# Queries of the expert retrieval in three passes over split operands, in a two-layer encoder kernel on one core

## What is computed

```python
def block(xb):                                   # per block of tokens, 8 heads
    q = (xb @ w_query).reshape(t, PEER_HEADS, 2, PEER_HALF).astype(jnp.float32)
    scores = jnp.einsum('thpd,hpnd->thpn', q, sk)        # 2 x 128 keys per head
    s_val, s_idx = lax.top_k(scores, PEER_TOPK)
    cand = s_val[:, :, 0, :, None] + s_val[:, :, 1, None, :]
    c_val, c_idx = lax.top_k(cand.reshape(t, PEER_HEADS, PEER_TOPK * PEER_TOPK), PEER_TOPK)
    ...                                          # expert = i1 * 128 + i2
    gate = jax.nn.softmax(c_val, axis=-1)
    act = jax.nn.gelu(jnp.einsum('thkd,td->thk', expert_u[expert], xb).astype(jnp.float32))
    coef = (gate * act).astype(xb.dtype)
    return jnp.einsum('thk,thkd->td', coef, expert_v[expert])
```

## Time and profile before

| | us |
|---|---|
| median of 3 runs | 2816.58 (2815.05 to 2818.69) |
| the profiled execution, its own time | 2819.95 |
| span in its profile | 2818.1 |
| TensorE busy | 2798.6 (99%) |
| VectorE busy | 2334.7 (83%) |
| ScalarE busy | 1050.3 (37%) |
| granted TensorE clock, mean | 0.997 |

### The profile page before, as it was taken

One profiled execution on the slowest core, in us unless ns is written; L12 is line 12 of the kernel. 1 busy time (PEld: TensorE's weight loads), 2 busy tenths in 40 slices (PEclk: granted clock), 3 DMA queues, 4 the chain that ended last, 5 costly groups with the idle time before them and its releaser, 6 DMA issues.

```text
span 2818.1 us, 40542 instructions
## 1 busy us (share of the span) xinstructions
PE 2798.6 (99%) x15010; PEld 1575.0 (56%) x15010; DVE 2334.7 (83%) x4382; ACT 1050.3 (37%) x1394; POOL 747.8 (27%) x519
## 2 busy tenths in 40 slices
PE   9999999999999999999999999999999999999999
PEld 5455555556666444444467775555566664444444
DVE  5954899997888899999843568999978889999996
ACT  2163323234555333333442442323345553333332
POOL 0000233421111445445200002333301114545450
PEclk9999999999999999999999999999999999999999
DMA  4213578776997999999702246878679979999993
GB/s 160 90 47 128 216 268 300 269 280 248 316 313 269 395 393 400 400 390 397 288 34 90 77 155 248 311 260 308 248 267 315 313 294 400 399 395 394 400 396 145
DMA packets 213943, 776.06 MB, mean 275 GB/s; under 512 B 14484, under 2 KB 101016, under 8 KB 193848
## 3 DMA queue, kind: packets, MB, share of 16 engines
q1 hardware_dynamic: 49200, 416.89, 38.6%
q0 software_dynamic: 73728, 268.47, 25.5%
q10 hardware_dynamic: 90888, 89.14, 9.4%
HBM read 681.90 MB, written 92.54 MB: 275 GB/s over the span
## 4 chain that ended last, share of the span: by engine, by line
PE 74%; issue 10%; PEld 8%; DVE 4%; DVEq 2%; ACT 1%; DMA 1%; PEldq 1%; POOL 0%; ACTq 0%; SPq 0%
PE ps L1983 15%; PE ps L1914 12%; PE ps L1913 12%; PE ps L1912 12%; PE ps L1886 8%; PEld ps L1983 8%; DVE arena L988 2%; PE ps L1588 2%; PE ps L1965 2%; PE ps L1964 2%; PE ps L1537 1%; PE ps L1538 1%; PE ps L1541 1%; DVEq L996 1%; PE ps L1922 1%
## 5 line engine op out<-in xcount | busy, mean ns | idle before, releaser
L1983 PE MATMUL ps<-arena 128*128 128x512 bf16 x4584 | 990.5, 379 | 1.7 <-DVE arena L1365 1.3
L521 POOL DMA_INDIRECT arena<-in_ur,arena x256 | 349.5, 1365 | 1548.7 <-DVE arena L1203 929.4
L1983 PEld LDWEIGHTS ps<-arena 128*128 128x128 bf16 x4584 | 448.2, 98 | 542.8 <-issue 1.7
L1176 DVE TENSOR_TENSOR arena<-arena 128x1024 bf16<-128x1024 f32 x512 | 611.7, 1220 | 117.0 <-ACT arena L767 95.3
L1914 PE MATMUL ps<-xnh,arena 128*128 128x384 bf16 x2048 | 667.6, 326 | 0.0
L1913 PE MATMUL ps<-xnl,arena 128*128 128x384 bf16 x2048 | 667.5, 326 | 0.0
L1912 PE MATMUL ps<-xnh,arena 128*128 128x384 bf16 x2048 | 667.4, 326 | 0.0
L767 ACT ACTIVATE arena<-arena 128x1024 bf16<-128x1024 f32 x512 | 524.7, 1048 | 122.8 <-PE ps L1983 99.6
L521 POOL DMA_INDIRECT arena<-in_v,arena x256 | 396.2, 1548 | 404.9 <-DVE x_res L1212 344.0
L1212 DVE SCALAR_TENSOR_TENSOR x_res<-arena,x_res 128x1024 f32<-128x1024 f32 x256 | 328.6, 1283 | 21.1 <-issue 0.9
L793 ACT ACTIVATE arena<-ps 128x384 f32<-128x384 f32 x256 | 125.6, 491 | 563.6 <-PE ps L1914 560.8
(11 more groups left out here) (250 smaller groups left out, 2544.8 us busy)
## 6 DMA issues: line engine op xcount, KB each, us to landing
arena<-in_v SPq DMA_DIRECT2D x64, 2048.0 KB
arena<-in_u SPq DMA_DIRECT2D x62, 2048.0 KB
h_scratch<-arena ACTq DMA_DIRECT2D x60, 768.0 KB
arena<-h_scratch SPq DMA_DIRECT2D x60, 768.0 KB
arena<-gate_scratch SPq DMA_DIRECT2D x64, 640.0 KB
arena<-in_wmix SPq DMA_DIRECT2D x14, 2048.0 KB, 7.9
gate_scratch<-xnT ACTq DMA_DIRECT2D x10, 2048.0 KB
gate_scratch<-arena ACTq DMA_DIRECT2D x10, 2048.0 KB
```

The lines of the kernel that those rows point to most:

```text
L521: pool.indirect_dma_start(ring[n % NBUF], None, ur_d[L] if g < P else vr_d[L], at).then_inc(gat_in[n % NBUF], 16)
L1176: dve.tensor_tensor(lo[:, s], raw[s // TPG][:, s % TPG], hi[:, s], ALU.subtract).then_inc(lo_ready, 1)
L1983: last = pe.matmul(ps[:, 2 + 2 * tt + dh], c, v[:, TPG * s + q, dh * 512:(dh + 1) * 512], start=start and c is ch and v is hi, stop=stop a ...
```

## The change

- The queries are made of rounded operands in three passes. x_hi (the rounded tokens) takes the place of xnT, x_rest (what is left) lies where x_res was. Before that, x goes to DRAM (x_keep, stored by ScalarE behind the norm's root, x_kept), and it is loaded again by SP after the last u group was asked for (x_back, waited for by VectorE at value group 4).
- The weights of a head are rounded by ScalarE into wq_hi (query_high: two activations of 128x1024, at the entry for head 0, then after the tile 8h + 4), and VectorE leaves the rest in the place of wq (query_low: two subtractions, in head h at a fixed place for head h + 1).
- TensorE makes per head 8 x 2 matmuls high x high and as many high x rest, in turn, and then 8 x 2 of low x high (high_tokens, low_weights). In head 0 the rests of tiles 2 and 3 are used only behind the first dense tile (rest_tokens), and the scores of head 0 come behind the second.
- norm_low and norm_high of tiles 1 to 3 write into xs; query_rest copies from there into x_hi and subtracts; the bf16 split reads xs too. For tile 0 the rests are eight operations out of PSUM.
- VectorE splits two tiles of u at once (split_two), except the first six of a layer.
- The one-hot rows are written two instructions in place of four, each twice as wide. Their order in the tile changes.

```diff
@@ -210,6 +212,10 @@
+        x_rest = rounded("x_rest", ARENA + KD * T + KD * TD, TT, KD, P)
+        wq_lo = rounded("wq_lo", A_X, KD, 2 * P)
+        wq_hi = [rounded("wq_hi0", A_X + 2304, KD, 2 * P)] + [rounded("wq_hi1", A_GR, KD, 2 * P)] * (PH - 1)
...
@@ -452,6 +463,10 @@
+                sp.wait_ge(q_done, PH * (L + 1))
+                for tt in range(TT):
+                    sp.dma_start(x[:, tt], x_keep[tt]).then_inc(x_back, 16)
...
@@ -548,6 +563,8 @@
+                if k % 2:
+                    act.dma_start(x_keep[tt], x[:, tt]).then_inc(x_kept[tt], 16)
...
@@ -766,8 +785,16 @@
+            def query_high(L, h):
+                act.wait_ge(wq_in, 16 * (PH * L + h + 1))
+                for p in range(2):
+                    at = slice(4 * p, 4 * p + 4)
+                    act.activation(wq_hi[h][:, at], wq[:, at], ACT.Copy).then_inc(q_high, 1)
+                query_high(L, 0)
...
@@ -834,6 +861,8 @@
+                    if n % RING == 4 and n < NK // 2 - RING:
+                        query_high(L, n // RING + 1)
...
@@ -925,15 +956,45 @@
+            def query_rest(k, tt):
+                at = slice(tt * P, (tt + 1) * P)
+                dve.wait_ge(xt_low, TT * k + tt + 1)
+                dve.drain()
+                if tt:
+                    src = xs[:, tt].rearrange("p (k t) -> p k t", t=P)
+                    dve.tensor_copy(x_hi[:, :, at], src).then_inc(x_top, 1)
+                    if tt == TT - 1:
+                        split_tile(tt)
+                    dve.wait_ge(x_kept[tt], 16 * (k // 2 + 1))
+                    dve.drain()
+                    dve.tensor_tensor(x_rest[:, tt], src, x_hi[:, :, at].bitcast(F32), ALU.subtract).then_inc(xt_rest, 1)
+                    return
+                dve.wait_ge(x_kept[tt], 16 * (k // 2 + 1))
+                for kd in range(KD):
+                    first = kd % (KD // 2) * P
+                    last = dve.scalar_tensor_tensor(x_rest[:, tt, kd], ps[:, turn_bank(k, tt) + kd // (KD // 2), first:first + P],
+                                                    cols[:, C_GAIN + KD * k + kd:C_GAIN + KD * k + kd + 1],
+                                                    x_hi[:, kd, at].bitcast(F32), ALU.mult, ALU.subtract)
+                last.then_inc(xt_rest, 1)
+            def query_low(L, h):
+                for p in range(2):
+                    at = slice(4 * p, 4 * p + 4)
+                    dve.wait_ge(q_high, 2 * (PH * L + h) + p + 1)
+                    dve.tensor_tensor(wq_lo[:, at], wq[:, at], wq_hi[h][:, at].bitcast(F32), ALU.subtract).then_inc(q_low, 1)
+            def split_tile(tt):
+                src, at = xs[:, tt].rearrange("p (k t) -> p k t", t=P), slice((tt - GT) * P, (tt - GT + 1) * P)
+                dve.tensor_copy(xnh[:, :, at], src)
+                dve.drain()
+                dve.tensor_tensor(xnl[:, :, at], src, xnh[:, :, at], ALU.subtract).then_inc(xn_split, 1)
-                if tt >= GT:
-                    dve.wait_ge(xt_low, TT * k + tt + 1)
-                    src, at = xnT[:, :, tt * P:(tt + 1) * P], slice((tt - GT) * P, (tt - GT + 1) * P)
-                    dve.drain()
-                    dve.tensor_copy(xnh[:, :, at], src)
-                    dve.drain()
-                    dve.tensor_tensor(xnl[:, :, at], src, xnh[:, :, at], ALU.subtract).then_inc(xn_split, 1)
+                query_rest(k, tt)
+                if GT <= tt < TT - 1:
+                    split_tile(tt)
...
@@ -947,6 +1008,8 @@
+                    if step == 2:
+                        query_low(m, 0)
...
@@ -1175,12 +1238,24 @@
+            def split_two(n, s, first):
+                if first is not None:
+                    dve.wait_ge(raw_in[s // TPG], first)
+                dve.wait_ge(hi_ready, n + 2)
+                at = slice(s % TPG, s % TPG + 2)
+                dve.tensor_tensor(lo[:, s:s + 2], raw[s // TPG][:, at], hi[:, s:s + 2], ALU.subtract).then_inc(lo_ready, 2)
-                    if n < TPG:
-                        dve.wait_ge(first_in[n], 16 * (L + 1))
-                    split_lo(T0 + n, n % RING, arrival(L, n) if n >= TPG and n % TPG == 0 else None)
+                    if n < AHEAD:
+                        if n < TPG:
+                            dve.wait_ge(first_in[n], 16 * (L + 1))
+                        split_lo(T0 + n, n % RING, arrival(L, n) if n == TPG else None)
+                    elif n % 2:
+                        n -= 1
+                        split_two(T0 + n, n % RING, arrival(L, n) if n % TPG == 0 else None)
...
@@ -1259,6 +1334,8 @@
+                    if h + 1 < PH:
+                        query_low(L, h + 1)
...
@@ -1397,6 +1474,7 @@
+                            dve.wait_ge(x_back, 16 * TT * (L + 1))
...
@@ -1466,6 +1544,8 @@
+                if k % 2 and tt == 2:
+                    pe.wait_ge(xt_rest, TT * (k - 1) + 1)
...
@@ -1881,22 +1961,44 @@
-                def queries(s, at):
+                def part(h, s, tiles):
+                    return slice(tiles.start * P, tiles.stop * P), slice(s * P, (s + 1) * P)
+                def high_tokens(h, s, tiles, rests):
+                    at, cols_at = part(h, s, tiles)
+                    pe.wait_ge(q_high, 2 * (PH * L + h + 1))
-                        last = pe.matmul(ps[:, 2 + s, at], wq[:, kd, s * P:(s + 1) * P], xnT[:, kd, at],
-                                         start=kd == 0, stop=kd == KD - 1)
+                        pe.matmul(ps[:, 2 + s, at], wq_hi[h][:, kd, cols_at], x_hi[:, kd, at], start=kd == 0, stop=False)
+                        if rests:
+                            rest_tokens(h, s, tiles, (kd,), False)
+                def rest_tokens(h, s, tiles, parts, stop):
+                    at, cols_at = part(h, s, tiles)
+                    bank = ps[:, 2 + s, at].rearrange("p (a t) -> p a t", t=P)
+                    for kd in parts:
+                        last = pe.matmul(bank, wq_hi[h][:, kd, cols_at], x_rest[:, tiles, kd], start=False,
+                                         stop=stop and kd == KD - 1)
-                halves = slice(0, T // 2), slice(T // 2, T)
-                pe.wait_ge(wq_in, 16 * (PH * L + 1))
-                pe.wait_ge(xt_low, TT * (2 * L + 1) + 2)
-                pe.wait_ge(xt_high, TT * (2 * L + 1) + 2)
-                queries(0, halves[0])
+                def low_weights(h, s, tiles, stop):
+                    at, cols_at = part(h, s, tiles)
+                    pe.wait_ge(q_low, 2 * (PH * L + h + 1))
+                    for kd in range(KD):
+                        last = pe.matmul(ps[:, 2 + s, at], wq_lo[:, kd, cols_at], x_hi[:, kd, at], start=False,
+                                         stop=stop and kd == KD - 1)
+                    return last
+                halves, every = (slice(0, TT // 2), slice(TT // 2, TT)), slice(0, TT)
+                pe.wait_ge(xt_rest, 2 * TT * L + 2)
+                high_tokens(0, 0, halves[0], True)
-                queries(1, halves[0])
-                all_turned(2 * L + 1)
-                queries(0, halves[1])
-                queries(1, halves[1]).then_inc(q_done, 1)
+                high_tokens(0, 1, halves[0], True)
+                low_weights(0, 0, halves[0], True)
+                low_weights(0, 1, halves[0], True)
+                pe.wait_ge(x_top, (TT - 1) * (L + 1))
+                for s in range(2):
+                    high_tokens(0, s, halves[1], False)
+                    low_weights(0, s, halves[1], False)
...
@@ -1924,14 +2026,20 @@
+                pe.wait_ge(xt_rest, 2 * TT * L + TT)
+                for s in range(2):
+                    last = rest_tokens(0, s, halves[1], range(KD), True)
+                last.then_inc(q_done, 1)
+                tile(0, 1)
-                for j in range(1, RING):
+                for j in range(2, RING):
-                    pe.wait_ge(wq_in, h * 16 + 16 * (PH * L + 1))
-                        last = queries(s, slice(0, T))
+                        high_tokens(h, s, every, True)
+                    for s in range(2):
+                        last = low_weights(h, s, every, True)
```

More of the change, by code:

```diff
@@ L168, in build @@
         picks = view(A_PICK, 3, TT, P)
-        pk = viewb(A_GR + TPG * TD, 4, TD)
+        pk = viewb(A_GR + TPG * TD, NB, 2, BT)
+        pg = viewb(A_GR + TPG * TD + TD, NB, 2, BT)
         ring = [view(A_RING + D * s, D) for s in range(NBUF)]
@@ L292, in build @@
         z_gain = sem("z_gain")
+        x_top = sem("x_top")
+        q_high = sem("q_high")
+        q_low = sem("q_low")
+        x_kept = [sem(f"x_kept{tt}") for tt in range(TT)]
+        x_back = sem("x_back")
         w_high = sem("w_high")
@@ L558, in norm_low @@
                 for kd in range(KD // 2):
-                    last = act.activation(xnT[:, kd, tt * P:(tt + 1) * P], ps[:, turn_bank(k, tt), kd * P:(kd + 1) * P], ACT.Copy,
+                    dst = xnT if k == 0 else x_hi
+                    dst = xs[:, tt, kd * P:(kd + 1) * P] if k and tt else dst[:, kd, tt * P:(tt + 1) * P]
```

(7 more changed lines are left out.)

33 lines of the change are left out of this document (17 added, 16 removed).

## The result

The kernel after takes **2839.78 us** (median of 4 runs, 2837.09 to 2843.04), the kernel before 2815.82 beside it: ratio 1.0081, 95% interval 1.0069 to 1.0094. It is slower by 24 us; the forecast was 12.7 faster. The profiled execution has a span of 2841.2 us against 2818.1.

The account below looks back on a forecast made before the run. TensorE bounds the kernel, VectorE 0.8 us per head behind. Two layers x 6.9, + 0.7, - 1.8 saves 12.7 us: 2819.95 to 2807.3, and 2803.9 as that execution is 3.4 above the median; range 2793 to 2818.

Parts of the forecast that it names:

- TensorE's head: Heads 1 to 7: queries in three rounded passes save TensorE 2.85 us per head, making its head 43.9 us.
- VectorE's head: Per head, low parts add 2.3 us and wide splits save 0.3, taking VectorE from 45.9 to 47.9 us.
- The reserve of 6.9: At TensorE's wait for q_low: 6.9 us of VectorE's lag is free, the rest stalls TensorE 13.1 us per layer.
- I cost it at nothing: Lag of 10.9 us at head 7: the shares, needed 11 us later, are met with nothing left over.
- The gain is the reserve: Heads of a layer: 20.0 us saved, 13.1 given back, 6.9 left; once VectorE sets the pace, shorter passes bring nothing.
- Entry of the layers: Layer 0 gains 0.7 us net; layer 1 loses 1.8, from 2.5 of added entry work (bounds 0 and 4.2).
- x stores: Four 512 KB stores per layer behind ScalarE's root, landing in 3.3 to 4 us, costed at nothing.
- Wide splits of v: Two-tile splits on VectorE save 0.3 us per head; pairing v was given no cost in the value phase.
- Reload: Behind the last u group: 2 MB of x takes 5.3 us, hidden in 7 free; otherwise TensorE waits up to 5.
- Clock: Rival: 4 us stalls in the heads drop the clock, 5.1 us more per layer, 2814 us; chance 0.20.
- VectorE dearer: Rival: VectorE's head grows 4.6 to 4.8 us over TensorE's, 2812 us; at 5.6, 2820; chance 0.12.
- the landing: Rival: stored token copies land late at the entries; 2815 us at 7.8 us landing, 2837 at 13.2; chance 0.16.

Follow-up runs that it names:

- e4: Kernel after plus 14 unused matmuls (3.2 us) ahead of the low pass of heads 4 to 7: 2840.37 us, ratio 1.0083.
- e10: Kernel after without VectorE's low parts for heads 1 to 7, third pass reads the high part again, 12 dots kept: 2814.86 us, ratio 0.9995.
- e6: e1 without the store of the tokens and the waits for it, reload reading the kernel's input: 2798.98 us, ratio 0.9945.
- e9: Kernel before with the paired splits and wider one-hot rows alone: 2818.98 us, ratio 1.0008.
- e11: Kernel after with single splits for v alone, pairs kept for u: 2834.97 us.
- e12: e8 with head 7 back at 4 dots (15 in the batches), single splits for v, reload after five of eight pairs of u loads: 2793.59 us.
- e16: e12 with the token reload spread, one tile behind each of four pairs of u loads: 2780.24 us, ratio 0.9864.
- e15: e12 with the reload of the tokens back behind the last u load: 2782.12 us, ratio 0.9871.
- e5: Kernel before with the dots moved as in e1, nothing else: 2816.91 us, ratio 1.0002.
- e1: Kernel after with 9 dots instead of 12 in heads 1 to 6, 8 moved ahead of the shares, 10 into the batches: 2800.93 us, ratio 0.9941.
- e8: e1 with moved dots 4 in head 7, 2 ahead of the shares, 12 in batches; two splits before the last stored tile's wait: 2790.62 us.

## Why the prediction was wrong, by its own steps

**TensorE's head** (2.85 saved, 43.9) and **VectorE's head** (47.9): right, measured 43.9 and 48.06. A wide split takes 2.29, the low part 1.22 twice. The waits are there too, five per layer instead of four: 0.36, 3.80, 2.36, 2.15 and 2.29, 11.0 in all against 13.1.

**The reserve of 6.9**: right as a length. In head 1 the low parts are done at 351.57 and TensorE comes to them at 358.38, 6.8 later. But the lag came sooner and was paid further. VectorE begins its top-k 3.0 us behind the scores in heads 0 and 1, 10.0 in head 2 and 12.1 in head 7:

```profile
374.74 1.22 DVE L1278 CUSTOM_DVE_ANT_0 arena<-arena 128x1024 f32<-128x1024 f32 x1 [2.85 <-DMA arena<-in_ur,arena]
375.89 1.64 DVE L1300 MAX8 arena<-arena 128x8 f32<-128x128 f32 x8
```

```profile
616.40 1.64 DVE L1300 MAX8 arena<-arena 128x8 f32<-128x128 f32 x8
```

By head 7 the lag is 27.9: six heads times 4.14, and 2.85 of waiting for gathered rows, for which the prediction had no term. Why the rows come late there no run separates. Of this the heads had paid 18.8 where the sum had 13.1, and 9.0 were still open where it had 10.9. The drops of the clock behind the stalls, 1.65 each, only shorten the next stall, as e4 shows.

**"I cost it at nothing"**, for the lag of 10.9 at head 7: the step that failed, and with it "The gain is the reserve". The sum charged the lag at one gate and took the rest as free. I looked at the shares alone, which VectorE met (its wait for them only fell from 9.07 to 7.21; by the rows its room there was 10.5, not 11), and not at the u loads, which start when VectorE has split a whole buffer. That gate took 5.5 and 5.2 us per layer, and e10 shows it bare. So of a lag of 24.0 the sum took 10.9 as free; of 27.9 only 3.5 were (3.8 in layer 1), and 24.4 were paid against 20.0 saved. Of the 35.8 us between forecast and measured spans this makes 22.2, the value phases 8.2, entries and startup the rest.

**Entry of the layers.** Layer 0 was to gain 0.7. TensorE idles 1.59 (1.6 said), but the rests of the last tile wait 3.92 for a store that landed 10.2 us after its issue among the u loads, and the first tile waits 2.81 and drops the clock. Layer 1 lost 4.2 by the end of the projection, where I took 2.5 and had 4.2 as the bound. The 2.5 was right for the waits: 0.64 and 2.44 where the kernel before has 0.57. The rest is the drop of the clock behind the 2.44 at 1650.07, which that term did not have. That the sum comes to the bound is luck.

**Costed at nothing.** x stores: 2 us (e6, no more than the spreads), right in size but for the place above. Wide rows: right, e9 shows no change. Wide splits of v: wrong, some 4 us per layer in the value phase (e11). Reload: not shown for the kernel after. VectorE waits 5.29 us for gathered rows at the start of the value phase there, but the kernel before has 4.4 in four waits at that place, without any reload. With single splits and e12's dots, spreading the reload shortened the two value phases by 1.4 and 2.6 us (e16 against e15).

**Rivals.** Clock: stalls of 2.1 to 3.8 us did drop it, for 3.4 us and not for 10, but in the heads that cost nothing of its own. The Trainium skill (TensorE: Matmul & The Clock Gate, section Why this matters for your kernels) advises against TensorE gaps of more than about 3 us between bursts of matmuls. Here 2.15 to 2.36 us were enough (layer 0, heads 5 to 7), and a wait of 3.42 in e5 left the clock up; the measurement decides. VectorE dearer: by 0.2 us a head only. The slow side was held by the landing and the dear VectorE; the case that came, nearly the whole of VectorE's lag paid, was not among them.

## What to carry to other kernels

When a change shortens the leading engine, look at the distance to the next one before its saving: here 0.8 of 2.85 us per head were to be had, and what was added to VectorE counted times the number of heads, all but 3 to 7 us per layer. A lag does not vanish at a gate that is met; follow it to every wait behind it, above all through a load whose issue waits for the late engine. Moving work out of the tight stretch (18 dots per layer) alone turned the same change from 0.8% slower to 0.6% faster (e1). With the moved dots placed better, single splits of v, two splits ahead of the store's landing and the reload spread, it is 1.4% faster (e16).

## What the runs showed of the hardware

- In the kernel after the clock fell to half for 3.4 us behind each of the 14 waits of TensorE of 2.1 us or more that follow the startup. Over all runs, from 200 us on, the length of the wait did not decide alone. From 1.4 to 1.86 us none lowered it. 1.87 in e11 (at 496.21) did; 3.10 in e15 (at 2310.62) and 3.42 in e5 (at 951.60) did not; each of 3.67 or more did. With the same matmuls around it, 2.48 in e1 at 1626.75 lowered it and 2.47 in e8 at 1623.50 did not.
- GpSimd's subtraction of 128x1024 with a rounded result takes 2.34 us, VectorE's 1.22.
- A 2 MB load lands 9.5 us after its issue with nothing ahead of it but a store of 768 KB; a store of 512 KB landed after 2.7 us in the median and 10.2 among loads.
